# A hybrid attention, SSD and mixture-of-experts layer: fourteen small experts, w_down in two transfers, up products on each fourth column

## The reference

```python
# moe_ffn(h, ...): 512 tokens, TOP_K = 4 of 32 experts
logits = (tok @ router_w + router_b)
top_vals, top_idx = lax.top_k(logits, TOP_K)
gate_w = jax.nn.softmax(top_vals, axis=-1)
gu = lax.ragged_dot(x_sorted, w_up, group_sizes) + b_up[e_sorted]   # w_up: 32 x 1024 x 2048
g, u = gu[:, :D_EXPERT], gu[:, D_EXPERT:]
g = jnp.minimum(g, SWIGLU_LIMIT)
u = jnp.clip(u, -SWIGLU_LIMIT, SWIGLU_LIMIT)
act = (u + 1.0) * (g * jax.nn.sigmoid(SWIGLU_ALPHA * g))
out = lax.ragged_dot(act, w_down, group_sizes) + b_down[e_sorted]   # w_down: 32 x 1024 x 1024
y = segment_sum(out * gate_w, token_of)
```

## Time and profile before

| | us |
|---|---|
| median of 3 runs | 1953.81 |
| lowest, highest | 1950.76, 1954.93 |
| the profiled execution | 1954.55 |
| its span in the trace | 1952.8 |
| granted TensorE clock, share | 0.995 |
| TensorE busy | 1900.5 (97%) |
| HBM read | 497.79 MB |

### The profile page before, as it was taken

How to read it: one execution, slowest core, us unless ns; L and a number is a source line. 1 busy time by engine, 2 the same in 40 slices (tenths; PEclk the granted TensorE clock), 3 DMA queues, 4 the chain that set the end, 5 groups by cost and what they waited for, 6 DMA issues and landing times.

```text
span 1952.8 us, 36539 instructions
## 1 busy us (share of the span) xinstructions
PE 1900.5 (97%) x15105; PEld 1133.9 (58%) x15105; DVE 708.9 (36%) x1104; ACT 482.3 (25%) x736; POOL 102.0 (5%) x137
## 2 busy tenths in 40 slices
PE   6999999999999999989999999999999999999998
PEld 4777788888888888834434434434343443444346
DVE  5666768887765445261001010000100000101066
ACT  3444443535535233211000101101010000010135
POOL 2000001001020000000000000000000000000030
PEclk9999999999999999989999999999999999999999
DMA  4333322222222443289999999999999999999862
GB/s 130 87 87 102 93 76 65 65 70 59 65 65 76 135 116 106 111 358 397 404 422 423 421 423 415 423 423 419 426 416 425 422 419 423 413 423 421 337 234 91
DMA packets 171462, 511.91 MB, mean 262 GB/s; under 512 B 14293, under 2 KB 125510, under 8 KB 138566
## 3 DMA queue, kind: packets, MB, share of 16 engines
q1 hardware_dynamic: 154480, 474.67, 62.2%
q10 hardware_dynamic: 9942, 18.50, 2.8%
q0 software_dynamic: 6912, 16.79, 2.4%
HBM read 497.79 MB, written 20.51 MB: 265 GB/s over the span
## 4 chain that ended last, share of the span: by engine, by line
PE 88%; DVE 4%; DMA 4%; ACT 2%; issue 1%; ACTq 0%; another core or an unknown queue 0%; DVEq 0%; SPq 0%
PE psum L2017 83%; DMA arena<-in_w_up 4%; PE psum L2408 2%; PE psum L2417 1%; DVE arena L1436 1%; PE psum L2079 0%; PE psum L2187 0%; PE psum L2147 0%; ACT w_hi L816 0%; PE psum L2132 0%; DVE w_lo L1320 0%; DVE residual L1946 0%; DVE arena L1504 0%; DVE arena L1350 0%; DVE arena L1415 0%
## 5 line engine op out<-in xcount | busy, mean ns | idle before, releaser
L2017 PE MATMUL psum<-arena 128*32 128x512 f32 (+5 forms) x10352 | 1049.9, 529 | 15.2 <-DVE arena L1436 5.5
L2017 PEld LDWEIGHTS psum<-arena 128*32 128x32 f32 (+2 forms) x10352 | 436.4, 116 | 579.5 <-issue 450.3
L1870 DVE TENSOR_SCALAR arena<-psum 128x768 f32<-128x768 f32 (+1 forms) x32 | 28.8, 899 | 914.3 <-ACT arena L1141 914.3
L2017 PE MATMUL psum<-h_hi,w_hi 128*128 128x512 f32 x640 | 258.8, 404 | 1.3 <-DVE w_lo L1320 1.3
L2017 PE MATMUL psum<-h_hi,w_lo 128*128 128x512 f32 x640 | 249.9, 391 | 0.0
L2017 PE MATMUL psum<-h_lo,w_hi 128*128 128x512 f32 x640 | 249.3, 390 | 0.0
L1320 DVE TENSOR_TENSOR w_lo<-arena,w_hi 128x1024 fp32r<-128x1024 f32 x104 | 135.7, 1305 | 187.7 <-ACT w_hi L816 186.7
L1141 ACT ACTIVATE arena<-psum 128x768 f32<-128x768 f32 (+1 forms) x32 | 24.4, 763 | 554.7 <-PE psum L2017 554.7
L2017 PEld LDWEIGHTS psum<-h_hi,w_hi 128*128 128x128 f32 x640 | 120.4, 188 | 34.6 <-issue 9.0
L2017 PEld LDWEIGHTS psum<-h_lo,w_hi 128*128 128x128 f32 x640 | 120.4, 188 | 26.5 <-issue 2.9
L2017 PEld LDWEIGHTS psum<-h_hi,w_lo 128*128 128x128 f32 x640 | 120.1, 188 | 25.8
(11 more groups left out here) (381 smaller groups left out, 1628.9 us busy)
## 6 DMA issues: line engine op xcount, KB each, us to landing
arena<-in_w_up SPq DMA_DIRECT2D x128, 2048.0 KB, 20.0
arena<-in_w_down SPq DMA_DIRECT2D x128, 1024.0 KB, 19.5
arena<-in_w_in SPq DMA_DIRECT2D x80, 512.0 KB, 3.9
arena<-in_w_ssd_branch SPq DMA_DIRECT2D x16, 512.0 KB, 4.1
y_dram<-arena ACTq DMA_DIRECT2D x24, 288.0 KB, 6.5
y_dram<-arena ACTq DMA_DIRECT2D x8, 512.0 KB, 4.0
arena<-in_w_attn_branch SPq DMA_DIRECT2D x8, 512.0 KB, 3.8
arena<-in_w_out SPq DMA_DIRECT2D x8, 512.0 KB, 4.3
```

Source lines behind the costliest of these rows:

```text
L1870: dve.tensor_scalar(u_sb[:, 0:n], up_psum[:, 0:n, 1, :], 1.0 + LIMIT, 1.0 - LIMIT, ALU.min, ALU.max).then_inc(u_ready, 1)
L2017: return pe.matmul(o, l, r, start=start, stop=stop)
```

## The change

`SMALLS` goes from 7 to 14, and small experts stand on each second place, 3, 5, ... 29. The sorting on VectorE finds sixteen smallest experts in two rounds of eight, and sixteen others in two rounds where it had three. `w_down` is loaded in two transfers of 2 MB, with four neighbouring rows of the matrix on one partition. The activations have to come in that order: row 4p + a of a half meets w_down's row a on partition p. So an up product now takes each fourth column of w_up (`up_set`, columns n with n mod 4 = s), the transposes of `hidden` take neighbouring columns, and the biases of w_up are stored in the same order (GpSimd and SP, at 26 to 35 and 146 to 156 us of the span).

```diff
-GROUP, SMALLS, FIRST_SMALL, PAIR = 4, 7, 3, 64
+SMALLS, FIRST_SMALL, PAIR = 14, 3, 64
+SIZE_BASE = EXPERTS * 128.0 * SEQ
...
-        w_dn_pair = [at(64 + 8 * c, 2, D) for c in range(KT // 2)]
-
-
-        up_both = [w.rearrange("p (u n) -> p u n", u=2) for w in (w_up_pair[k // 2][:, k % 2, :] for k in range(KT))]
+        w_dn_four = [at(64 + 16 * c, 4, D) for c in range(2)]
+
+
+        up_set = [w.rearrange("p (u n s) -> p s u n", u=2, s=4) for w in (w_up_pair[k // 2][:, k % 2, :] for k in range(KT))]
...
-        w_dn_d = w_down[0].rearrange("e (c p a) n -> e c p a n", p=P, a=2)
+        w_dn_d = w_down[0].rearrange("e (c p a) n -> e c p a n", p=P, a=4)
...
             def load_down(i, expert):
-                for c in range(KT // 2):
+                for c in range(2):
                     if not isinstance(i, int) or i:
-                        sp.wait_ge(down_used, KT * (i - 1) + 2 * c + 2)
-                    sp.dma_start(w_dn_pair[c], w_dn_d[ds(expert, 1), c].rearrange("e p a n -> (e p) a n")
+                        sp.wait_ge(down_used, KT * (i - 1) + 4 * c + 4)
+                    sp.dma_start(w_dn_four[c], w_dn_d[ds(expert, 1), c].rearrange("e p a n -> (e p) a n")
                                  ).then_inc(rows_landed[c], 16)
...
-            own.then(dve.scalar_tensor_tensor(out=key[0], in0=last[0:1, 0, sorted_of], scalar=-float(EXPERTS * P),
-                                              in1=iota_far[0:1, sorted_of], op0=ALU.mult, op1=ALU.add))
-            own.then(dve.max(smallest[0:1], key[0]))
+            own.then(dve.tensor_scalar(key[2], last[0:1, 0, sorted_of], -float(EXPERTS * P), SIZE_BASE, ALU.mult, ALU.add))
+            own.then(dve.tensor_tensor(key[0], key[2], iota_far[0:1, sorted_of], ALU.add))
+            own.then(dve.max(smallest[0:1, 0:8], key[0]))
+            own.mark(dve.max_index(small_at[0:1, 0:8], smallest[0:1, 0:8], key[0]))
+            own.then(dve.scalar_tensor_tensor(out=key[1], in0=key[0], scalar=smallest[0:1, 7:8], in1=key[0],
+                                              op0=ALU.is_lt, op1=ALU.mult))
+            own.then(dve.max(smallest[0:1, 8:16], key[1]))
             own.then(dve.scalar_tensor_tensor(out=owner[0:1, 31:32], in0=smallest[0:1, SMALLS - 1:SMALLS],
-                                              scalar=-float(EXPERTS * P * PAIR + P), in1=inc[0:1, EXPERTS - 1:EXPERTS],
-                                              op0=ALU.is_lt, op1=ALU.add))
+                                              scalar=SIZE_BASE - float(EXPERTS * P * PAIR + P),
+                                              in1=inc[0:1, EXPERTS - 1:EXPERTS], op0=ALU.is_lt, op1=ALU.add))
             dve.tensor_copy(control[:, FLAG:FLAG + 1], owner[0:1, 31:32]).then_inc(tables_ready, 1)
-            own.mark(dve.max_index(small_at[0:1], smallest[0:1], key[0]))
-            own.then(dve.scalar_tensor_tensor(out=key[1], in0=key[0], scalar=smallest[0:1, SMALLS - 1:SMALLS],
+            own.mark(dve.max_index(small_at[0:1, 8:16], smallest[0:1, 8:16], key[1]))
+            own.then(dve.scalar_tensor_tensor(out=key[2], in0=key[0], scalar=smallest[0:1, SMALLS - 1:SMALLS],
                                               in1=iota_far[0:1, sorted_of], op0=ALU.is_lt, op1=ALU.mult))
             own.mark(dve.tensor_copy(small_of[0:1], small_at[0:1]))
-            own.then(dve.max(others[0:1, 0:8], key[1]))
+            own.then(dve.max(others[0:1, 0:8], key[2]))
             own.mark(dve.tensor_scalar(small_of[0:1], small_of[0:1], 2.0, None, ALU.add))
-            own.then(dve.scalar_tensor_tensor(out=key[2], in0=key[1], scalar=others[0:1, 7:8], in1=key[1],
+            own.then(dve.scalar_tensor_tensor(out=key[1], in0=key[2], scalar=others[0:1, 7:8], in1=key[2],
                                               op0=ALU.is_lt, op1=ALU.mult))
-            own.then(dve.max(others[0:1, 8:16], key[2]))
-            own.then(dve.scalar_tensor_tensor(out=key[1], in0=key[2], scalar=others[0:1, 15:16], in1=key[2],
-                                              op0=ALU.is_lt, op1=ALU.mult))
-            own.then(dve.max(others[0:1, 16:24], key[1]))
+            own.then(dve.max(others[0:1, 8:16], key[1]))
             own.then(dve.tensor_scalar(other_of[0:1], others[0:1], -1.0 / P, float(EXPERTS - 1), ALU.mult, ALU.add))
-            by_group = control[:, 4:4 + GROUP * SMALLS].rearrange("o (q c) -> o q c", c=GROUP)
-            dve.tensor_copy(by_group[:, :, 0:3], other_of[0:1, 0:21].rearrange("o (q c) -> o q c", c=3))
-            dve.tensor_copy(control[:, 2:3], other_of[0:1, 21:22])
-            dve.tensor_copy(control[:, FIRST_SMALL:FIRST_SMALL + GROUP * SMALLS].rearrange(
-                "o (q c) -> o q c", c=GROUP)[:, :, 0], small_of[0:1, 0:SMALLS])
+            dve.tensor_copy(control[:, 2:4 + 2 * SMALLS].rearrange("o (q c) -> o q c", c=2)[:, :, 0],
+                            other_of[0:1, 0:SMALLS + 1])
+            dve.tensor_copy(control[:, FIRST_SMALL:FIRST_SMALL + 2 * SMALLS].rearrange("o (q c) -> o q c", c=2)[:, :, 0],
+                            small_of[0:1, 0:SMALLS])
...
-                    ins = pe.transpose(turned_act[:, k, :], hidden[:, k // 2 * QUARTER + k % 2:(k // 2 + 1) * QUARTER:2], ident[:])
+                    ins = pe.transpose(turned_act[:, k, :], hidden[:, k * P:(k + 1) * P], ident[:])
...
-                               up_both[k][:, :, r * QUARTER:(r + 1) * QUARTER], k == 0, False)
-                        ins = mm(bank(r)[strip(STRIPS)], x_T[:, k, strip(order[r])], up_both[k][:, :, WIDE:FF],
+                               up_set[k][:, r], k == 0, False)
+                        ins = mm(bank(r)[strip(STRIPS)], x_T[:, k, strip(order[r])], up_set[k][:, STRIPS],
...
-                                         up_both[k][:, :, c * QUARTER:(c + 1) * QUARTER], k == 0, False)
+                                         up_set[k][:, c], k == 0, False)
...
-                    pe.wait_ge(rows_landed[k // 2], 16 * (i + 1) + 48)
+                    pe.wait_ge(rows_landed[k // 4], 16 * (i + 1) + 48)
...
-                    w = w_dn_pair[k // 2][:, k % 2, :]
+                    w, at_k = w_dn_four[k // 4][:, k % 4, :], 2 * (k % 4) + k // 4
...
-            def place(b, c):
-                round_of(b, small=c == 1, small_behind=c == 2)
+            def pair(b):
+
+                round_of(b, small=True)
+                round_of(b + 1, small_behind=True)
```

More of the change, by code:

```diff
@@ L350, in build @@
         by_size = at(RT, 3, EXPERTS, extra=26 * P)
-        smallest, others = at(RT, 8, extra=26 * P + 96), at(RT, 24, extra=26 * P + 104)
-        small_at = arena[:, kb(RT) + 27 * P:kb(RT) + 27 * P + 8].bitcast(U32)
-        small_of, other_of = at(RT, 8, extra=27 * P + 8), at(RT, 24, extra=27 * P + 16)
+        smallest, others = at(RT, 16, extra=26 * P + 96), at(RT, 16, extra=26 * P + 112)
+        small_at = arena[:, kb(RT) + 27 * P:kb(RT) + 27 * P + 16].bitcast(U32)
+        small_of, other_of = at(RT, 16, extra=27 * P + 16), at(RT, 16, extra=27 * P + 32)
         slot_hot = at(MOE_AT + 25, TT * TOPK * CAP // 2).bitcast(F16).rearrange("p (n s) -> p n s", s=CAP)
@@ L695, in _ @@
             pool.wait_ge(fills_ready, 2)
-            own.then(pool.tensor_scalar(bias_src[:, 0:512], bias_src[:, 0:512], one_of_u[:], None, ALU.add))
-            own.then(pool.tensor_copy(bias_part[:, 0, :], bias_src))
-            own.then(pool.tensor_tensor(bias_rest, bias_src, bias_part[:, 0, :], ALU.subtract))
-            own.then(pool.tensor_copy(bias_part[:, 1, :], bias_rest))
-            own.then(pool.tensor_tensor(bias_rest, bias_rest, bias_part[:, 1, :], ALU.subtract))
-            pool.tensor_copy(bias_part[:, 2, :], bias_rest).then_inc(bias_parts_ready, 1)
+            own.then(pool.tensor_scalar(bias_all[:, 0:512].rearrange("p (s n) -> p n s", s=4),
+                                        bias_src.rearrange("p (n s) -> p n s", s=4), one_of_u[:], None, ALU.add))
+            own.then(pool.tensor_copy(bias_part[:, 0, :], bias_all))
+            own.then(pool.tensor_tensor(bias_all, bias_all, bias_part[:, 0, :], ALU.subtract))
+            own.then(pool.tensor_copy(bias_part[:, 1, :], bias_all))
+            own.then(pool.tensor_tensor(bias_all, bias_all, bias_part[:, 1, :], ALU.subtract))
+            pool.tensor_copy(bias_part[:, 2, :], bias_all).then_inc(bias_parts_ready, 1)
             def masks(g, c):
@@ L1195, in _ @@
             swish(1)
-            with act.Fori(2, 2 + GROUP * SMALLS, GROUP) as b:
-                for c in range(GROUP):
-                    copy_act(b + c - 1, small=c == 2)
-                    expert_out(b + c - 2, small=c == 3)
-                    swish(b + c, small=c == 1)
-            copy_act(EXPERTS - 3)
-            expert_out(EXPERTS - 4)
-            swish(EXPERTS - 2)
+            copy_act(1)
+            expert_out(0)
+            swish(2)
+            copy_act(2)
+            expert_out(1)
+            swish(FIRST_SMALL, small=True)
+            copy_act(FIRST_SMALL, small=True)
```

(32 more changed lines are left out.)

40 lines of the change are left out of this document (20 added, 20 removed).

## The result

| | before | after |
|---|---|---|
| median, us | 1953.91 | 2496.16 |
| lowest, highest | 1950.76, 1954.93 | 2495.18, 2496.54 |
| ratio, 95% interval | | 1.278, 1.276 to 1.280 |

The changed kernel is 28% slower. The forecast was 1943.5 us with a range to 1956, so it was wrong in sign and by 553 us. What happened is the first rival, in its heavy half.

A forecast was written before the change was run, and what follows sets the result against it. The DMA was taken as already the slower, at 32.0 us per expert. Sorting 0.35, shorter stores -2.2, long rows -3.1 and tail -5.6 gave -10.6 us: forecast 1943.5 us, own range 1938 to 1949, 8-in-10 range 1936 to 1956.

The forecast's parts named there:

- the first rival: Expert stage: strided reads slow the up product, making the kernel slower; chance 0.08 for 5 to 17%, 0.13 for more.
- its heavy half: Up products slowed beyond 17%: 2140 us at 1.49 times, about 2430 at twice as long; chance 0.13.
- The stride: Up products reading each fourth column: zero cost taken, as four cycles a column leave the reader time.
- The page: Skill page on SBUF's 16-byte lines: speaks against the stride; by it the result would be the first rival's.
- Its threshold: Up products in the expert stage: slowing up to 17% is hidden but for the tail, 1 us per cent there.
- The slack of 6 us: Expert stage: TensorE has 63.5 - 57.5 = 6 us of slack per pair of a small and a full expert.
- The sum by the DMA alone: Expert stage: nearly all 73 us TensorE saves become waiting for w_up; a pair costs TensorE 57.5 us, DMA 64.0.
- The long rows of w_down: w_down loads with 16 KB rows instead of 8: 3.1 us gained, 0.10 per expert.
- The tail: From the last w_up chunk's landing to the last product's end: 33.0 us instead of 38.6, 5.6 us gained.
- The hair: Tail: expert 31's first w_down half lands barely in time at L + 18.3; if late, at most 2.5 us lost.
- The sorting: VectorE's expert sorting between slot table and row table: one added index search, 0.35 us more, all counting.
- The transposes: Transposes of hidden now read neighbouring columns instead of each second: a small gain, given no term in the sum.

The follow-up runs named there:

- the kernel with neighbours: Changed kernel with up products streaming neighbouring columns instead of each fourth, w_down still in two transfers (doesn't compute the layer): 1942.56 us.
- the doses: Kernel with up products on pairs of neighbouring columns, but one, then two of eight w_up row blocks read at each fourth column again: 1980.51 and 2055.70 us.
- one block: Kernel with up products on pairs of neighbouring columns, but one of eight w_up row blocks read at each fourth column again: 1980.51 us.
- two blocks: Kernel with up products on pairs of neighbouring columns, but two of eight w_up row blocks read at each fourth column again: 2055.70 us.
- the pairs: Changed kernel with up products on pairs of neighbouring columns and transposes on each second column, w_down still in two transfers: 1949.51 us.
- fourteen alone: Kernel before with only the fourteen small experts added; w_down in four transfers, streams and transposes as before: 1943.90 us.
- the second of these kernels: Second kernel of products alone, layer left out, varying how columns fall on 16-byte lines: fp32 fours took 20.93 us from column 0, 26.00 from column 1.

## Why the prediction was wrong, point by point

- **The stride: the step that failed.** "I take zero for the products: ... 1.7 ns or four cycles of 2.4 GHz for a column, so the reader has time." In its place the runs show 3.55 ns for a visit to a line, and with one column per line that is more than the 1.69 ns of a column. The up products grew by 574 us where the term was zero, and undoing the stride takes 2496.16 - 1942.56 = 554 us off the kernel. The duration per column was read rightly, but it says nothing of how long a slower read would take: no row showed that. The only row on a stride, showed 1.49 times, at a stride of two, on the other operand. It gave the direction and not the size (a streamed operand pays 1.05 at a stride of two and 2.1 at four). I set it aside by an argument that had no row at all.
- **The page.** By the Trainium skill, "SBUF — State Buffer" ("Door 1: The DMA port swizzle"), an access on a new 16-byte line is penalised and two hits in a line give full speed. The runs agree for fp32: one hit 2.1 times, two hits 1.05. The rule deserved more than a chance of 0.21. For bf16 the measurement says otherwise, two hits are too few: stride four, two hits in a line, took 11.13 us against 5.36, and four neighbours in each eighth column, four hits, 5.82.
- **The first rival** was right in kind. Its price at twice the length, "about 2430", counts 60 us for the unpaired experts and the tail. At the measured 2.1 it becomes 1943.5 + 15 x (1.1 x 34.75 - 6) + 66 = 2493; measured are 2496. That is in part luck: there are 14 pairs and not 15, and the slack is smaller than it says. Its threshold was wrong: 18% more (24.70 + 16.39 against 34.75) gave 1980.5 us, and by the text it would have been about 1966. The slack of 6 us was counted in fifteen pairs, 90 us; the kernel with neighbours waits 58.6 us for w_up, and that is what there is. With it the doses come out to about 10 us: one block adds 18 x 3.89 + 14 x 2.45 = 104 us of up products to that kernel, less 59 is 45 (measured 38), two blocks add 178, less 59 is 119 (measured 113), the whole stride 623, less 59 is 564 (measured 554). The slack isn't used up before anything shows, though: the pairs add 32 us, still wait 31.3, and cost 7.
- **The sum by the DMA alone.** This was right. TensorE's pair of 57.5 us is there in fourteen alone until the DMA catches up (down products at 973.06 and 1030.57). Then its full up products come every 1292.22 - 1228.53 = 63.7 us, forecast 64.0, and 57 of the 73 us became waiting for w_up.
- **The long rows of w_down**, 3.1 us gained. Neighbours against fourteen alone is 1942.56 against 1943.90; intervals overlap. Not settled, and at most a few us.
- **The tail.** Fourteen alone, the last w_up chunk (issue, then landing) and the last products:

```profile
L556 SPq DMA_DIRECT2D arena<-in_w_up x1: 333/333/333, 1821.9 to 1821.9; - x1
...
DMA to landing us min/median/max: 24.5/24.5/24.5
```

```profile
1865.05 14.11 PE L2026 MATMUL psum<-arena 128*96 128x512 f32 x48 [0.90 <-ACT arena L1168]
1879.09 0.63 PE L2026 MATMUL psum<-arena,ones_bf 32*96 32x512 bf16 x2
```

It lands at 1821.9 + 24.5 = 1846.4, and the last product ends at 1879.7, 33.3 us later; 33.0 was forecast, 38.6 was before. With two transfers of w_down, in the kernel with neighbours, the last product starts so:

```profile
1859.15 14.38 PE L2027 MATMUL psum<-arena 128*96 128x512 f32 x48 [2.76 <-DMA arena<-in_w_down]
```

It waits 2.76 us for w_down where 0.90 us for the activations had been the limit. The hair that the prediction named was missing, and it costs 1.9 us, inside the 2.5 given for it. This kernel's last w_up chunk lands at 1814.3 + 24.3 = 1838.6 us, some 6 us ahead of the forecast 1845, and its last product ends 35.5 us later and not 33.0. The two errors have opposite signs, and the landing belongs to an execution of 1940.09 us, the fastest of the four; so the total of the forecast sum was nearer than its parts.
- **The sorting.** VectorE's timeline of the changed kernel, then TensorE's first up product:

```profile
852.88 0.21 DVE L1827 TENSOR_SCALAR slot_token<-psum 96x53 uint32<-96x53 f32 x1
...
859.03 0.17 DVE L1869 CAST rows_u<-arena 128x16 uint32<-128x16 f32 x1
860.16 0.96 DVE L1874 COPY arena<-psum 128x768 f32<-128x768 f32 x1 [0.96 <-DVE rows_u L1869]
```

```profile
861.17 43.65 PE L2027 MATMUL psum<-arena 128*32 128x512 f32 x192 [2.07 <-DVE arena L1874]
```

From the slot table to the row table it is 859.03 - 852.88 = 6.15 us, 0.38 more than in the earlier trace rows (0.35 forecast), and the first up product starts 0.51 us later.
- **The transposes** of hidden, whose stride the change took away: 0.88 us for six, 0.99 before. Loading one of their blocks takes 140 ns in the changed kernel, 209 before. It is the gain that was left at zero, 0.1 us an expert.

```profile
908.95 0.88 PE L2427 MATMUL psum<-ident,arena 128*128 128x128 f32 x6 [2.21 <-DVE arena L1888]
```

- **Chances.** 0.13 for the heavy stride came from weighing an argument against a row. With the earlier trace rows and the Trainium skill on one side and no row on the other, it should have been much larger.

## What to carry to other kernels

Before an operand's layout is changed, count how many streamed columns fall into each 16-byte line in the order in which they are read, and measure the product alone in a small kernel. Four hits in a line cost at most 9% here in fp32 and bf16, two hits 5 to 7% in fp32 and 2.1 times in bf16. Where two resources look full, look at landing times: here TensorE's time counted in full until the DMA had caught up, and hardly after. A duration per element is no proof that a slower operand would be hidden in it.

## What was not expected of the hardware

- A single visit to a line costs 3.55 ns in fp32, whose products stand twice in the profile (192 entries for 96 products), and 21.86 us / 24 / 512 = 1.78 ns in bf16, where they stand once. So it is about 1.78 ns for each entry and line in both.
- fp32r doesn't follow this: 11.04 us with a stride of two, 11.25 with four, 10.53 with eight, against 6.53 and, in the second of these kernels, 5.73 for neighbours. Any gap costs it about 1.7 to 2.0 times, and wider ones no more. Why is open.
- A DMA share of 1.00 at 409 to 414 GB/s still had reserve: full queues moved 423 to 425. The landing times (7.8 us from a nearly empty queue, 10.9 with some reserve, 26 when full) told what the share did not.
